# The gated delta rule of a two-block model: from two chains over pairs of tiles to four chains over single tiles

## The reference, cut to what matters

```python
def step(s, inp):
    r_t, w_t, k_t, v_t, a_t, b_t = inp
    sa = jnp.einsum('bhvk,bhk->bhv', s, a_t)
    s = s * w_t[:, :, None, :] + sa[..., None] * b_t[:, :, None, :] + v_t[..., None] * k_t[:, :, None, :]
    y = jnp.einsum('bhvk,bhk->bhv', s, r_t) if emit else None
    return s, y
...
y = ys[0] + ys[1]
mu = jnp.mean(y, axis=-1, keepdims=True)
var = jnp.mean(jnp.square(y - mu), axis=-1, keepdims=True)
yn = ((y - mu) * lax.rsqrt(var + RW_GN_EPS)).reshape(bsz, l, RW_WIDTH) * lnx_g + lnx_b
yn = yn + (bonus[0] + bonus[1]).reshape(bsz, l, RW_WIDTH)
g = jax.nn.sigmoid(gd) @ g2
return (yn * g).astype(r.dtype), (states[0], states[1])
```

## Time and profile before

| what | us |
|---|---|
| median of 3 runs (3947.62 to 3955.78) | 3949.37 |
| span of the profiled execution, first to last instruction | 3941.6 |
| `rwmix`, first instruction to the first of the next stage | 587.0 |
| PE busy in the span | 3377.2 |
| DVE / ACT / POOL busy in the span | 2360.6 / 1768.8 / 731.1 |

### The profile page before, as it was taken

How to read it: one execution, slowest core, us unless ns; L and a number is a source line. 1 busy time by engine, 2 the same in 40 slices (tenths; PEclk the granted TensorE clock), 3 DMA queues, 4 the chain that set the end, 5 groups by cost and what they waited for, 6 DMA issues and landing times. The chain is left out here.

```text
span 3941.6 us, 97846 instructions
## 1 busy us (share of the span) xinstructions
PE 3377.2 (86%) x38463; PEld 2331.6 (59%) x38463; DVE 2360.6 (60%) x4245; ACT 1768.8 (45%) x2361; POOL 731.1 (19%) x706
## 2 busy tenths in 40 slices
PE   4999799677778587979998998999689999878789
PEld 0899788577677475733332333333267777666567
DVE  1688688655555466627776766776377574056631
ACT  0577577422222124307776766776222321156620
POOL 4000000043444200331221221222112333200000
PEclk7999899899899788989999999999899999988899
DMA  8354445421221255949889999953734323265452
GB/s 315 84 171 139 160 130 166 159 86 46 61 72 44 82 167 200 209 155 315 277 263 356 351 354 357 326 160 76 244 87 128 86 75 96 95 153 132 117 181 75
DMA packets 520291, 665.36 MB, mean 169 GB/s; under 512 B 77168, under 2 KB 423984, under 8 KB 516768
## 3 DMA queue, kind: packets, MB, share of 16 engines
q1 hardware_dynamic: 494576, 572.44, 45.2%
q0 software_dynamic: 25216, 86.62, 8.9%
q10 hardware_dynamic: 48, 0.05, 0.0%
HBM read 493.08 MB, written 165.94 MB: 167 GB/s over the span
## 5 line engine op out<-in xcount | busy, mean ns | idle before, releaser
L2600 PE MATMUL routed_p_gu<-routed_fixed,routed_x 128*32 128x512 f32 x3840 | 572.5, 600 | 0.0
L2600 PE MATMUL routed_p_gu<-moe_exp_w,routed_x 128*32 x1280 | 571.5, 600 | 0.7 <-DVE routed_fixed L2722 0.7
L2654 ACT COPY routed_fixed<-moe_exp_w 128x1024 f32 x320 | 332.6, 1047 | 222.1 <-DMA moe_exp_w<-in_exp_w_up_dram 86.3
L2722 DVE COPY routed_fixed<-moe_exp_w 128x1024 f32 x640 | 398.0, 681 | 51.3 <-DMA moe_exp_w<-in_exp_w_up_dram 42.9
L544 PE MATMUL front_ps<-front_a_high,front_w_high 128*128 128x320 f32 (+1 forms) x1120 | 362.7, 324 | 16.3 <-DVE front_w_low L797 13.4
L544 PE MATMUL front_ps<-front_a_low,front_w_high 128*128 128x320 f32 (+1 forms) x1120 | 353.8, 316 | 0.0
L544 PE MATMUL front_ps<-front_a_high,front_w_low 128*128 128x320 f32 (+1 forms) x1120 | 353.7, 316 | 0.0
L2600 PEld LDWEIGHTS routed_p_gu<-moe_exp_w,routed_x 128*32 128x32 f32 x1280 | 135.4, 111 | 356.2 <-issue 356.2
L3606 PE MATMUL pre_ps<-pre_a_high,pre_w_high 128*128 128x512 f32 x720 | 287.1, 399 | 13.3 <-ACT pre_xb L3753 6.7
L2615 PE MATMUL routed_p_y<-routed_wd,routed_hT 128*32 x640 | 290.4, 597 | 3.4 <-ACT routed_fixed L2665 3.4
L2615 PE MATMUL routed_p_y<-routed_fixed,routed_hT 128*32 128x512 f32 x1920 | 291.4, 597 | 0.0
(11 more groups left out here) (550 smaller groups left out, 7386.6 us busy)
## 6 DMA issues: line engine op xcount, KB each, us to landing
moe_exp_w<-in_exp_w_gate_dram SPq DMA_DIRECT2D x64, 1024.0 KB, 13.3
moe_exp_w<-in_exp_w_up_dram SPq DMA_DIRECT2D x64, 1024.0 KB, 16.4
routed_wd<-in_exp_w_down_dram SPq DMA_DIRECT2D x64, 1024.0 KB, 15.1
front_wt<-in_w_in_dram SPq DMA_DIRECT2D x70, 512.0 KB, 4.4
mod_w<-in_w_mod_dram SPq DMA_DIRECT2D x24, 1024.0 KB, 18.2
pre_wt<-in_w_in_dram SPq DMA_DIRECT2D x44, 512.0 KB, 4.0
out_a<-mix SPq DMA_DIRECT2D x24, 512.0 KB, 4.0
total<-out_none SPq DMA_DIRECT2D x24, 512.0 KB
```

What stands on the lines that cost most here:

```text
L2600: op = nc.tensor.matmul(p_gu[spot(s), :], x[:, b % 2, k, spot(s)], w, start=(k == 0), stop=(k == KD - 1))
L2654: nc.scalar.copy(fixed[:, place_of(b, c), 0, :], wgu[:, bass.ds(e % WS, 1), c * D:(c + 1) * D].rearrange("p o n -> p (o n)"))\
L2722: op = nc.vector.tensor_copy(fixed[:, place_of(b, c), s - 1, :], wgu[:, bass.ds(es[s] % WS, 1), c * D:(c + 1) * D].rearrange("p o n -> p ( ...
```

## The change

`rwkv_mix` is written anew. All four groups run at once as four chains (`GROUPS = QT`), each with two PSUM banks. A unit is now one tile of 128 tokens in each direction: 8 problems, two chunk steps per direction, ten units per chain and forty in all. `interleaved` gives each engine, per round, the steps of chains 0 to 3 at places s, s - 6, s - 12, s - 18 (`OFFSET = 6`).

- A unit has 24 slots: `turn, lay, rest0, prod, masked, rest1, t0, w1, t1, ..., w5, t5, as0, vn0, st0, as1, vn1, st1, rest2`. `rest0`, `rest1` and `rest2` hold no work on any engine.
- The matrices m, nn and q are gone. For each chunk step, PE multiplies a with the state (`as`), DVE adds the part within the chunk (`rest`), PE applies the inverse (`vn`), ACT copies the result beside v, and PE makes the state's increment with 128 rows of stacked b and k at once (`st`); DVE adds the decayed state, which POOL makes (`faded`). Outputs come from 16 matmuls of the unit at the end of `st1`.
- a is no longer transposed. b and v are turned and copied by ACT, k by DVE (`keys`). In the levels the second set of matmuls is gone; from level 2 on, PE turns T by two 128x128 transposes, which ACT copies to TT before DVE may read W.
- Masks are applied in pieces of 256 columns, `at` and `bkT` on 64 partitions each.
- The normalization is done per unit of 2x128 tokens in the last four units of each chain: eight slots, `mean` to `gate`, lie between the levels of the following unit, and after the tenth unit alone. Units 7, 8 and 9 so have 32 slots, and 8 follow. With the offsets this makes 272 places and 290 rounds.
- Loads: per unit and direction one DMA for a, r, b, and four for halves of k and v (64 partitions, 256 bytes each); the decays are loaded once for the whole stage, into `tot`. ACT, DVE and POOL wait at their start for `once`, the four DMAs that SyncE issues after the 40 loads of the first four units.

```diff
-    PAIRS = TILES // 2
-    UNITS = 2 * PAIRS
+    GROUPS = QT
+    LAST = TILES - 1
...
-    OFFSET = 11
+    OFFSET = 6
...
+            out = ["turn", "lay", "rest0", "prod", "masked", "rest1", "t0"] + norm[0:1]
+            for l in range(1, LEVELS + 1):
+                out += [f"w{l}"] + norm[2 * l - 1:2 * l] + [f"t{l}"] + norm[2 * l:2 * l + 1]
+            return out + ["as0", "vn0", "st0", "as1", "vn1"] + ["st1", "rest2"]
...
+            for s in range(len(order) + OFFSET * (GROUPS - 1)):
+                for u in range(GROUPS):
...
+                    sp.dma_start(src[u][:, z, :, d, :], rw["abrk"][d, 0:3, rows, tk].rearrange("j p t -> p j t"))\
+                        .then_inc(loaded[u][z], 16)
+                    for c in range(2):
+                        tk = slice(a * P + c * HEAD, a * P + (c + 1) * HEAD)
+                        sp.dma_start(kv[u][:, z, K, d, half(1 - c)], rw["k"][d, rows, tk]).then_inc(loaded[u][z], 16)
+                        sp.dma_start(kv[u][:, z, V, d, half(1 - c)], rw["v"][rows, tk]).then_inc(loaded[u][z], 16)
...
+            for u in range(GROUPS):
+                load(0, u)
+            for d in range(2):
+                sp.dma_start(tot[:, :, d, :], rw["tot"][d].rearrange("(u p) c -> p u c", p=P)).then_inc(once, 16)
...
+                def turned_inverse():
+                    for e in range(2):
+                        op = nc.tensor.transpose(b[:, 0, span(TT_AT + e * P, P)], T[u][:, 2 * e:2 * e + 2, :], consts["ident"][:, :])
...
+                    if l > 1:
+                        turned_inverse()
+                    PO.wait(pe, by_pool[u], n, f"x{l}")
...
+                elif p[:2] == "as":
...
+                    for s, d, c, h in problems((s,)):
+                        op = nc.tensor.matmul(b[half(c), h, span(REST_AT, HEAD)], x[half(h), A, d, half(c)], S[u][half(h), z, s, d, :],
+                                              start=True, stop=True)
...
+                elif p[0] == "w":
+                    PE.wait(dve, products[u], n, p)
+                    if int(p[1]) > 1:
+                        AC.wait(dve, by_scalar[u], n, f"tt{p[1]}")
...
+                def first_level(c, h):
+                    pool.drain()
+                    nc.gpsimd.tensor_tensor(TT[u][half(h), :, c, :], at[u][half(c), h::2, :],
+                                            consts["rw_mask"][half(c), MASK_LEVEL, h::2, :], ALU.mult)
...
+            pool.wait_ge(once, 64)
```

More of the change, by code:

```diff
@@ L1038, in pe_steps @@
+            if n == TILES:
+                return back
+            out = ["turn", "prod", "t0"]
             for l in range(1, LEVELS + 1):
[L1039 to L1042 removed]
+                out += [f"w{l}"] + (back if l == 3 else []) + [f"t{l}"]
@@ L1044, in dve_steps @@
+            return out + ["as0", "vn0", "st0", "as1", "vn1", "st1"]
         def dve_steps(n):
-            out = ["tb", "at", "cb", "bk", "ck"]
+            norm = ["mean", "var", "norm"] if finishing(n) else []
+            if n == TILES:
+                return norm
+            out = ["keys", "at", "bk", "cc"] + norm[0:1]
             for l in range(1, LEVELS + 1):
-                out += [f"w{l}", f"tt{l}"]
-            out += ["wup", "m", "n", "c0"] + (["q"] if latent(n) else []) + ["c1", "c2"]
@@ L1049, in dve_steps @@
-            out += ["c3"] if not last(n) else []
-            return out + (["y"] if latent(n) else []) + (["mean", "var", "norm"] if last(n) else [])
+                out += [f"w{l}"] + norm[l:l + 1]
+            return out + ["as0", "st0", "as1"] + (["st1"] if n < LAST else []) + (["y"] if latent(n) else [])
         def act_steps(n):
-            out = ["ta", "tk", "tv", "zed", "t0"] + [f"t{l}" for l in range(1, LEVELS)]
-            return out + ["wup"] + (["y"] if latent(n) else []) + (["square", "root", "back"] if last(n) else [])
@@ L1056, in pool_steps @@
[L1056 to L1061 removed]
+            norm = ["square", "root", "res"] if finishing(n) else []
+            if n == TILES:
+                return norm
+            out = ["turn", "lay", "t0"]
```

641 lines of the change are left out of this document (297 added, 344 removed).

## The result

The changed kernel takes 3901.22 us (median of 4 runs, 3899.21 to 3908.04); the kernel before, on the same chip, takes 3948.53 (median of 4). The ratio is 0.9879, 95% interval 0.9865 to 0.9893: 48 us less. The forecast was 3883, 18 us too low, inside its range of 3830 to 3965. Of the runs further down, one of the nine executions of `turns_twice` ran at a granted clock of 0.811 and took 4162.78 us, and the ratios leave it out.

What follows compares the result with a forecast made beforehand. A round lasts as long as its slowest member, an engine's sum or one chain's path. Start 24, ordinary units 322, long units 150, last rounds 29, ramp -9, end 4.5 made 520.5 us against 587.0, so 3883 us; range 3830 to 3965.

Steps and rivals of the forecast that it cites:

- the line through three sizes: POOL's price, 0.18 us plus 2.1 ns a column, fitted to 256, 512 and 1024 columns.
- factor of 1.055: Multiplier on an ordinary unit's 43.6 us of summed rounds in `rwmix`, giving 46.0 us.
- the maxima: Each round of `rwmix` priced by its slowest engine sum or chain path; 24 rounds sum to 43.6 us.
- my two bounds: Ordinary unit in `rwmix`: 43.6 us with no factor, 48.3 us with the old order's factor of 1.11.
- the upper bound: Price of PE's matmuls with 128 rows (`st`, new outputs): 0.058 us each, the lower bound being 0.033.
- The first 18 run with one to three chains, 0.5 less each: -9: Start of `rwmix`: the first 18 rounds, with fewer chains, each take 0.5 us less, 9 us in all.
- the forecast's own case: Stage `rwmix` with a factor from 1.0 (3852 us) to 1.17 (3935 us); chance 0.57.
- The table: The list of round kinds in `rwmix` with slowest members: 10.9 us per six rounds, 43.6 for 24.
- rival 3: POOL sets the round in `rwmix`: small pieces cost 0.723 us, `faded0` comes late; 44 us slower, 3993; chance 0.10.
- (1) Better overlap: Units in `rwmix` take 39.4 us, long ones 45; 128 us saved, 3821 us; chance 0.15.
- (2) The rounds eat the gain: Factor 1.2 in `rwmix`, ordinary unit 52.3 us, long one 57; no change, 3949 us; chance 0.13.
- (4) The clock: Clock low all through `rwmix`, PE's 31.3 us nearer 60 a unit; kernel over 4050 us; chance 0.05.

Runs made afterwards that it cites:

- turns_twice: The changed kernel with the two transposes of each level from 2 on made twice; ratio 0.9956 to the kernel before, 30 us more than the change.
- keys_act: The changed kernel with the turned keys copied by ACT instead of DVE; ratio 0.9960 to the kernel before, 32 us more than the change.
- once_first: The changed kernel with the four DMAs of `once` issued before the 40 first loads; ratio 0.9847 to the kernel before, 13 us less than the change.
- offset8: The changed kernel with chains eight rounds apart instead of six; ratio 1.0100 to the kernel before, 87 us more than the change.
- merged: The changed kernel with normalization steps put into the levels' slots, so units 7 to 9 have 24 slots; ratio 0.9885 to the kernel before.
- together: The changed kernel with `once` loaded first, POOL's masks spread over the slots and normalization in the levels' slots; 3887.05 us, ratio 0.9843 to the kernel before.
- no_rests: The changed kernel without its three empty slots `rest0`, `rest1`, `rest2`; ratio 1.0069 to the kernel before, 75 us more than the change.
- no_rest2: The changed kernel without the empty slot `rest2` only, 23 slots; ratio 1.0138 to the kernel before, 102 us more than the change.

## Why the prediction was right, and where not

**The direction holds, and the mechanism in the main.** The period was to be 46.0 and is 46.7. The prices of ACT, DVE and POOL came out within 0.02 us: 128 columns on POOL 0.452 (0.45 from the line through three sizes), 64 columns 0.306 (0.31), 256 columns on ACT 0.373 (0.363), on DVE 0.421 (0.42). The factor of 1.055 over the maxima is 46.7/43.6 = 1.07, between my two bounds. That DVE's W would wait for ACT's TT is the largest wait there is, 119.9 us in 116. `keys_act` and `once_first` moved the time as the same arithmetic says; `turns_twice` moved the period by half of what it says, and `offset8` the time by twice. No run stands between the two kernels, so how much of the 38.9 us comes from PE's smaller work and how much from four chains instead of two is worked out here, not measured.

**The matmuls with 128 rows**, for which I took the upper bound of 0.058 us, show in two bursts of the same length (timeline of PE, 8 and 16 records, so 4 and 8 matmuls):

```profile
897.33 0.32 PEld L1216 LDWEIGHTS rwmix_ps<-rwmix_T,rwmix_X 64*64 64x64 f32 x16 [0.17 <-issue]
897.34 0.46 PE L1216 MATMUL rwmix_ps<-rwmix_T,rwmix_X 64*64 64x64 f32 x16
...
897.73 0.46 PE L1258 MATMUL rwmix_ps<-rwmix_uv,rwmix_bk 128*64 128x64 f32 x8
```

Less the tail of 0.22 that is 0.24/8 = 0.03 for the one and 0.24/4 = 0.06 for the other: the upper bound was right.

**The sum** missed by 27.6 us in the stage. By pieces, forecast and measured (the tenth unit after its identity, with the last 26 rounds, is one piece; the identity stands in a unit's fourth round, and the forecast's terms are divided there; rounding makes them 520.8 in all):

| piece | forecast | measured | difference |
|---|---|---|---|
| first DMA to first copy (772.8 to 796.2) | 24 | 23.4 | -0.6 |
| to the second unit's identity (852.4) | 41.7 | 56.2 | +14.5 |
| six ordinary units | 276.0 | 280.0 | +4.0 |
| two long units | 100.2 | 105.4 | +5.2 |
| last identity to POOL's end (1237.8 to 1315.5) | 74.4 | 77.7 | +3.3 |
| end | 4.5 | 5.4 | +0.9 |

The step that failed is "The first 18 run with one to three chains, 0.5 less each: -9". It was a guess with no row behind it, and with 14.5 of the 27.6 us it is over half of the miss. Timeline of POOL, the identities of chains 1, 2, 3 in their first unit:

```profile
816.85 0.72 POOL L1447 TENSOR_TENSOR rwmix_TT<-rwmix_TT,eye 128x256 f32<-128x256 f32 x1
829.26 0.72 POOL L1447 TENSOR_TENSOR rwmix_TT<-rwmix_TT,eye 128x256 f32<-128x256 f32 x1
841.20 0.73 POOL L1447 TENSOR_TENSOR rwmix_TT<-rwmix_TT,eye 128x256 f32<-128x256 f32 x1
```

Each step from one chain's identity to the next is six rounds, and the next chain starts in its middle. The steps take 13.5 us with one chain and then two (803.34 to 816.85), 12.4 with two and three, 11.9 with three and four, 11.2 with four; in the steady state six rounds take 11.7. The term gave 1.4 us to a round of this ramp. With few chains a round is one chain's path alone, and that is no shorter than a full round. The clock adds to it, 0.74 until 838 against 0.97 in the first 38 us of work before. The same burst at the two clocks, PE's timeline:

```profile
805.08 1.06 PE L1186 MATMUL rwmix_ps<-ident,rwmix_kv 128*128 128x128 f32 x4
...
830.59 0.60 PE L1186 MATMUL rwmix_ps<-ident,rwmix_kv 128*128 128x128 f32 x4
```

The traces part the clock from the rest. The second and third step in the change (columns as in the earlier trace rows):

```profile
816.90:829.30 12.40, 9.57 (x240) 7.74 (x240) 5.23 (x14) 5.95 (x18) 6.03 (x11) 0.86 0.01 3
829.30:841.20 11.90, 9.71 (x262) 7.62 (x262) 6.33 (x20) 6.54 (x20) 7.02 (x14) 1.00 0.08 23
```

and the same second step in `once_first`, whose order of work there is the same:

```profile
803.60:817.30 13.70, 11.84 (x256) 9.42 (x252) 5.23 (x14) 6.17 (x18) 6.03 (x10) 0.67 0.47 120
```

At the full clock the third step still takes 11.9 us where the term gave 10.0, so the term fails without the clock too.

PE's 27.3 us of the ramp at 0.74 would be about 27.3 x 0.74 = 20.2 at the full clock, so the clock explains at most 7 of the 14.5. From the first copy to the second identity it is 56.2 us at a clock of 0.78 in the change and 57.6 at 0.71 in `once_first` (57.8 at 0.71 in `merged`): 1.5 us for 0.07, by which 0.22 would be some 5, an estimate from these three traces. Chains that start one by one leave PE idle a third of the ramp (busy 27.3 of 41.8). At the other end the clock is 0.79 too, with PE busy 58 of 77.7. The old order had two chains to start, and no such ramp. I had the clock as a rival for the whole stage, not as a price of its ends.

The long units cost 52.7, not 50.1; `merged` brings them to 50.7 without their extra rounds, and `together` to 50.8. The price of the start was 44 x 0.505 plus 2.4, which is 24.6 and stands in the sum as 24; 23.4 was measured. The lower end of the forecast's own case is a slip as well: a factor of 1.0 takes 24.6 us off the ten units and gives 3858, not 3852.

**From stage to median.** 3.6 us more were gained outside the stage, in parts whose code is the same. And the forecast put the median 7.8 above the span, as before; here it is 2.1, since the execution profiled for the kernel before seems to have lain below its median (the profile gives no time of its own beside it). 27.6 less 3.6 less 5.7 is the 18 of the median.

**Priced at nothing: the empty rounds.** The table priced a round by what is in it, an empty one by its neighbours', and so would have had `no_rests` and `no_rest2` faster or little slower. They cost 75 and 102 us to leave out. What the table lacks is not an engine's sum but the order of jobs on POOL and the banks taken over from one step to the next. The forecast was near because at 24 slots and an offset of 6 these collisions hardly occur. I had looked at POOL's queue for `faded0` alone (rival 3), and had not laid its jobs out for other offsets; that they do not meet here was luck.

**The rivals.** (1) Better overlap, 39.4 a unit: nothing moved the period below 46.1. (2) The rounds eat the gain: no; and `merged` shows that a round as such costs next to nothing. (3) POOL: wrong in the price (128 and 64 columns follow the line) and right as a mechanism, which `offset8` and `no_rest2` bring out with up to 5.3 and 3.5 us an instance. Its margin here is small, 2.6 us late at most, and one slot away from deciding. (4) The clock: 1.00 through the ordinary units (the third of the stretches above), with a quarter of PE's work in transposes (12.7 of the 53.0 us of its groups there, overlaps counted twice), and `turns_twice` kept it with more. The Trainium skill, "TensorE: Matmul & The Clock Gate", section on PE-mode transpose, says that the full clock does not engage for transposes, which do not count as PE being busy in the same way; nothing in these runs shows a loss from that, though no run had transposes alone.
